# Fourteen weight low parts moved to GpSimd in the conv stage, ten native strips made split strips

## What is computed

```python
h = layer_norm(x) * (1.0 + sc1[:, None]) + sh1[:, None]
proj = h @ w_in[l]
a_val, a_gate, u_pool, gate_a, gate_b = jnp.split(proj, ...)
ya = a_val * jax.nn.sigmoid(a_gate)
ya = causal_dwconv(ya, w_dw_a[l], b_dw_a[l])            # 31 taps, 512 channels
ya = jax.nn.silu(layer_norm(ya, ln_a_g[l], ln_a_b[l]))
ya = ya @ w_pw_a[l]
pooled = causal_multiscale_pool(u_pool)                 # window means over 2, 4, 8, 16 tokens, minus u_pool
yb = jnp.einsum("bsgc,gcd->bsgd", pooled, w_pool[l]).reshape(bsz, s, D_MODEL) * pool_scale[l]
merged = jax.nn.sigmoid(gate_a) * ya + jax.nn.sigmoid(gate_b) * yb
mix = merged @ w_out[l]
```

## Time and profile before

| what | value |
|---|---|
| time, median of three runs | 828.81 us (828.03 to 829.47) |
| time of the profiled execution | 828.66 us |
| its span, first to last instruction | 826.9 us |
| TensorE busy | 811.2 us, 98% of the span |
| VectorE busy | 661.9 us, 80% |
| ScalarE busy | 456.8 us, 55% |
| GpSimd busy | 43.4 us, 5% |
| mean granted TensorE clock | 0.997 |

### The profile page before, as it was taken

One profiled execution on the slowest core, in us unless ns is written; L12 is line 12 of the kernel. 1 busy time (PEld: TensorE's weight loads), 2 busy tenths in 40 slices (PEclk: granted clock), 3 DMA queues, 4 the chain that ended last, 5 costly groups with the idle time before them and its releaser, 6 DMA issues.

```text
span 826.9 us, 14985 instructions
## 1 busy us (share of the span) xinstructions
PE 811.2 (98%) x5394; PEld 738.3 (89%) x5394; DVE 661.9 (80%) x1043; ACT 456.8 (55%) x682; POOL 43.4 (5%) x58
## 2 busy tenths in 40 slices
PE   9999999999999999999999999999999999999995
PEld 9898999988778999999988789988988999999884
DVE  5979887786966887787868778999898888888566
ACT  6464545565646665657565636115744777776440
POOL 0009000000011000000000000060000000000000
PEclk9999999999999999999999999999999999999998
DMA  6957675679735747383749572446571665565641
GB/s 223 363 201 265 209 260 190 238 253 361 256 139 166 261 147 268 119 285 111 271 170 335 183 254 106 136 150 212 187 248 58 229 202 182 192 209 207 201 154 51
DMA packets 49002, 170.57 MB, mean 206 GB/s; under 512 B 6080, under 2 KB 6720, under 8 KB 48960
## 3 DMA queue, kind: packets, MB, share of 16 engines
q1 hardware_dynamic: 40896, 143.23, 50.5%
q10 hardware_dynamic: 8064, 26.78, 9.3%
HBM read 168.93 MB, written 1.06 MB: 206 GB/s over the span
## 4 chain that ended last, share of the span: by engine, by line
PE 77%; DVE 13%; ACT 4%; issue 4%; DMA 1%; DVEq 1%; ACTq 0%
PE bank L498 12%; PE bank L500 12%; PE bank L499 12%; PE bank L566 8%; PE bank L568 8%; PE bank L567 8%; DVE bank L2011 4%; DVE wlo L1521 3%; PE bank L512 2%; PE bank L703 2%; PE bank L704 2%; PE bank L705 2%; DVE ada_raw L1533 1%; PE bank L609 1%; PE bank L852 1%
## 5 line engine op out<-in xcount | busy, mean ns | idle before, releaser
L990 ACT ACTIVATE whi<-raw 128x1024 fp32r<-128x1024 f32 (+1 forms) x236 | 244.2, 1041 | 198.3 <-PE bank L500 85.3
L1521 DVE TENSOR_TENSOR wlo<-raw,whi 128x1024 fp32r<-128x1024 f32 (+1 forms) x236 | 282.9, 1211 | 66.3 <-ACT whi L990 64.2
L498 PE MATMUL bank<-H,whi 128*128 128x256 f32 x816 | 230.8, 283 | 0.6 <-DVE wlo L1521 0.4
L499 PE MATMUL bank<-H,whi 128*128 128x256 f32 x816 | 227.7, 279 | 0.0
L500 PE MATMUL bank<-H,wlo 128*128 128x256 f32 x816 | 227.7, 279 | 0.0
L498 PEld LDWEIGHTS bank<-H,whi 128*128 128x128 f32 x816 | 153.8, 189 | 2.1 <-issue 1.2
L499 PEld LDWEIGHTS bank<-H,whi 128*128 128x128 f32 x816 | 154.7, 190 | 0.1
L500 PEld LDWEIGHTS bank<-H,wlo 128*128 128x128 f32 x816 | 153.2, 188 | 0.0
L566 PE MATMUL bank<-whi,Y 128*128 128x512 f32 x216 | 84.9, 393 | 0.3 <-DVE wlo L1521 0.3
L568 PE MATMUL bank<-whi,Y 128*128 128x512 f32 x216 | 84.3, 390 | 0.0
L567 PE MATMUL bank<-wlo,Y 128*128 128x512 f32 x216 | 84.2, 390 | 0.0
(11 more groups left out here) (265 smaller groups left out, 1315.2 us busy)
## 6 DMA issues: line engine op xcount, KB each, us to landing
ada_raw<-ada_in ACTq DMA_DIRECT2D x48, 512.0 KB, 5.2
raw<-w_head SPq DMA_DIRECT2D x47, 512.0 KB, 4.5
raw<-w_up SPq DMA_DIRECT2D x42, 512.0 KB, 3.5
raw<-w_down SPq DMA_DIRECT2D x22, 512.0 KB, 3.4
raw<-w_uq SPq DMA_DIRECT2D x24, 384.0 KB, 3.1
raw<-w_ret_out SPq DMA_DIRECT2D x16, 512.0 KB, 5.1
raw<-w_mla_gate SPq DMA_DIRECT2D x16, 512.0 KB, 4.6
raw<-w_mla_out SPq DMA_DIRECT2D x16, 512.0 KB, 5.3
```

What stands on the lines that cost most here:

```text
L498: mm(o, whi[:, s, c], a[:, 0, :], start=start, stop=False)
L499: mm(o, whi[:, s, c], a[:, 1, :], start=False, stop=False)
L990: activation(parts_of(b + (per * i if isinstance(i, int) else 0), n)[0], block_in(b, n), ACT.Copy).then_inc(hi_done, 1)
L1521: tt(lo, block_in(b, n), f32(hi), ALU.subtract).then_inc(lo_done, 1)
```

## The change

- WP2, WP3 and WG0 to WG7 become split strips, so that all 20 strips of `B_WP` and `B_WG` are. SyncE loads them without waiting for TensorE.
- Their high parts go to ScalarE, two ahead of each evacuation.
- The low parts of 14 blocks (`GIVEN`: WP2, WP3, WG0 to WG11) go to GpSimd. It makes five, then the window mean over 2, four, the mean over 4, five, and then the means over 8 and 16.
- VectorE loses the low parts of WG8 to WG11 (three between the last taps, one behind `conv_sum`) and the `skip_split`. Behind `conv_sum` it waits until GpSimd has made all of its parts and makes that of WG12; that of WG13 comes behind the centring, and `Sl` moves behind the scaling by `rstd`.
- TensorE does `conv_mean` after WG12 (before: after WG10) and `conv_squares` after WG14 (before: after WG12).
- ScalarE makes `Sh` between the root and the SiLU table (before: between two evacuations).
- The squares lie in `SGT` instead of in `WK`.

```diff
+GIVEN = [B_WP + 2 + j for j in range(14)]
...
             load_all(B_WP, "pool_in")
-            load_plain_loop(B_WG, "gates", 3, 4)
-            load_some(B_WG, "gates", 12, 16)
+            load_all(B_WG, "gates")
...
-                if j < 2:
-                    strip(B_WP + j, halves(b)[j % 2], H)
-                else:
-                    plain_tokens(B_WP + j, halves(b)[j % 2])
-            with pe.Fori(0, 2) as i:
-                for j in range(4):
-                    if j % 2 == 0:
-                        b = free_a(A_WG + j // 2, 2, i)
-                    plain_tokens(B_WG + j, halves(b)[j % 2], 4, i)
-            for j in range(8, 16):
+                strip(B_WP + j, halves(b)[j % 2], H)
+            for j in range(16):
                 if j % 2 == 0:
                     b = free_a(A_WG + j // 2)
                 strip(B_WG + j, halves(b)[j % 2], H)
-                if j == 10:
+                if j == 12:
                     conv_mean()
-                if j == 12:
+                if j == 14:
                     conv_squares()
...
             split(B_WA + 6)
-            skip_split(10)
+            split(B_WA + 7)
             value_gate(3)
             act.wait_ge(pads, 1)
-
+            split(B_WP)
+            split(B_WP + 1)
             evac(B_WP + 1, 0, U[:, 0:2, 16:16 + T], ACT.Copy)
+            split(B_WP + 2)
+            split(B_WP + 3)
             evac(B_WP + 3, 1, U[:, 2:4, 16:16 + T], ACT.Copy)
-            for n in range(3):
+            for n in range(6):
+                split(B_WG + 2 * n)
+                split(B_WG + 2 * n + 1)
                 evac(B_WG + 2 * n + 1, n, pair(G, n), ACT.Sigmoid)
-            act.wait_ge(pooled, 4)
-            activation(Sh, PO, ACT.Copy).then_inc(pooled_hi, 1)
...
             activation(root[:], M3[:, 0:T], ACT.Sqrt, bias=col("ln_eps"), scale=1.0 / (4 * P)).then_inc(root_done, 1)
+            act.wait_ge(pooled, 4)
+            activation(Sh, PO, ACT.Copy).then_inc(pooled_hi, 1)
             table(ACT.Silu)
...
             for k in range(4):
                 if k < 3:
-                    split(B_WG + 5 + k)
-                if k < 3:
                     taps(0, (28 + k,))
...
             tt(CS[:, 0, :], CS[:, 0, :], CS[:, 1, :], ALU.add).then_inc(conv_sum, 1)
-            split(B_WG + 8)
+            dve.wait_ge(lo_done, RING + GIVEN[-1] + 1)
             split(B_WG + 9)
-            split(B_WG + 10)
...
                 stt(pair(Z, p), over(M2[:, 0:T], 2), -1.0 / (4 * P), pair(CO, p), ALU.mult, ALU.add).then_inc(centred, 1)
+            split(B_WG + 10)
...
+            def low_part(b):
+
+                hi, lo = parts_of(b)
+                pool.wait_ge(hi_done, b + 1)
+                gtt(lo, block_in(b, 1024), f32(hi), ALU.subtract).then_inc(lo_done, 1)
...
+            pool.wait_ge(lo_done, RING + GIVEN[0])
+            for n, b in enumerate(GIVEN):
+                low_part(b)
+                if n == 4:
+                    pool.wait_ge(act_free, A_WP + 2 + 2)
+                    window_mean(0)
+                if n == 8:
+                    window_mean(1)
+            window_mean(2)
+            window_mean(3)
```

More of the change, by code:

```diff
@@ L198, in program @@
         SQ = WK[:, 8:16, :]
+        SQC = flat(SGT[:]).rearrange("p (a t) -> p a t", a=4)
         Q, K = WK[:, 0:2, :], WK[:, 2:4, :]
@@ L625, in conv_squares @@
                 for k in range(2):
-                    last = mm(M3[:, 0:T], ones[:], SQ[:, k, :], start=(k == 0), stop=(k == 1))
+                    last = mm(M3[:, 0:T], ones[:], SQC[:, k, :], start=(k == 0), stop=(k == 1))
                 last.then_inc(stat_ready, 1)
@@ L1384, in _ @@
             split(B_WA + 6)
-            skip_split(10)
+            split(B_WA + 7)
             value_gate(3)
             act.wait_ge(pads, 1)
+            split(B_WP)
+            split(B_WP + 1)
             evac(B_WP + 1, 0, U[:, 0:2, 16:16 + T], ACT.Copy)
+            split(B_WP + 2)
+            split(B_WP + 3)
             evac(B_WP + 3, 1, U[:, 2:4, 16:16 + T], ACT.Copy)
-            for n in range(3):
+            for n in range(6):
+                split(B_WG + 2 * n)
+                split(B_WG + 2 * n + 1)
                 evac(B_WG + 2 * n + 1, n, pair(G, n), ACT.Sigmoid)
-            act.wait_ge(pooled, 4)
-            activation(Sh, PO, ACT.Copy).then_inc(pooled_hi, 1)
[L1395 to L1398, removed]
-            split(B_WG + 8)
[L1400 to L1403, removed]
             for p in range(2):
                 act.wait_ge(centred, p + 1)
-                activation(pair(SQ, p), pair(Z, p), ACT.Square).then_inc(sq_ready, 1)
+                activation(pair(SQC, p), pair(Z, p), ACT.Square).then_inc(sq_ready, 1)
             table(ACT.Sqrt)
@@ L2076, in _ @@
                 stt(pair(Z, p), over(M2[:, 0:T], 2), -1.0 / (4 * P), pair(CO, p), ALU.mult, ALU.add).then_inc(centred, 1)
+            split(B_WG + 10)
+            dve.wait_ge(sq_ready, 2)
+            tt(pair(SQC, 0), pair(SQC, 0), pair(SQC, 1), ALU.add).then_inc(conv_sum, 1)
             split(B_WG + 11)
-            dve.wait_ge(sq_ready, 2)
-            tt(pair(SQ, 0), pair(SQ, 0), pair(SQ, 1), ALU.add).then_inc(conv_sum, 1)
-            dve.wait_ge(pooled_hi, 1)
-            tt(Sl, PO, f32(Sh), ALU.subtract).then_inc(pooled_ready, 1)
             split(B_WG + 12)
-            split(B_WG + 13)
             dve.wait_ge(centred, 2)
@@ L2089, in _ @@
                 tt(pair(Z, p), pair(Z, p), over(rstd[:], 2), ALU.mult).then_inc(t_ready, 1)
+            dve.wait_ge(pooled_hi, 1)
+            tt(Sl, PO, f32(Sh), ALU.subtract).then_inc(pooled_ready, 1)
+            split(B_WG + 13)
             split(B_WG + 14)
@@ L2328, in _, with window_mean @@
             pool.wait_ge(pads, 1)
-            pool.wait_ge(act_free, A_WP + 2 + 2)
-            for g, window in enumerate(WINDOWS):
+            def low_part(b):
+                hi, lo = parts_of(b)
+                pool.wait_ge(hi_done, b + 1)
+                gtt(lo, block_in(b, 1024), f32(hi), ALU.subtract).then_inc(lo_done, 1)
+            def window_mean(g):
                 src, shift, n = U[:, g, :], 1, 0
-                while shift < window:
+                while shift < WINDOWS[g]:
                     lo = 2 * shift - 1
@@ L2338, in _ @@
                 chained(gtt(src[:, 16:32], src[:, 16:32], cnt[:, g, :], ALU.mult))
-                chained(gts(src[:, 16:16 + T], src[:, 16:16 + T], 1.0 / window, None, ALU.mult))
+                chained(gts(src[:, 16:16 + T], src[:, 16:16 + T], 1.0 / WINDOWS[g], None, ALU.mult))
                 gtt(PO[:, g, :], src[:, 16:16 + T], U[:, g, 16:16 + T], ALU.subtract).then_inc(pooled, 1)
                 pool.wait_ge(pooled, g + 1)
+            pool.wait_ge(lo_done, RING + GIVEN[0])
[8 more added lines that the diff above has]
+            window_mean(3)
 def _features(a):
```

## The result

| | before | after |
|---|---|---|
| median of 14 runs each, us | 828.57 (824.41 to 829.47) | 832.21 (828.0 to 834.77) |
| ratio, 95% interval | | 1.0045 [1.0032, 1.0059] |
| profiled execution, us | 828.66, span 826.9, clock 0.997 | 829.87, span 828.1, clock 0.995 |
| first strip of the stage to PW0, us | 509.20 to 591.20: 82.00 | 508.18 to 592.46: 84.28 |
| PW0 to the end of the span, us | 235.7 | 235.6 |

The change makes the kernel slower, by 3.6 us between the medians, where 2.3 was forecast. The comparison of the two profiled executions does not show the whole of it. The profiled execution of after is one of the quickest of its 14, and its conv stage began 1.02 us earlier than in the profile of before, in code that the change doesn't touch. So I measure every profile from the stage's first strip to PW0.

A forecast was written before the change was run, and what follows sets the result against it. It took the conv stage as balanced between TensorE and VectorE, with the chain behind the sum of taps deciding. 828.66 + 1.0 (chain) - 0.1 (root to evacuation) + 1.4 (collisions) = 830.96, stated as 831.1 us, range 828.5 to 836.0.

The forecast's parts named there:

- the signs that were named: Conv stage: low parts 2.3 to 2.5 us, second sum ending 569 to 569.5, waits over 2 us, root near 583.
- a sign of being wrong: End of conv stage: root before 580, mean without wait, low parts over 2.6 us, or clock under 1 behind WG12.
- TensorE's 7.2 us come back as waits: Ten exchanged strips' saving returns as waits: 1.5 us WG7, 2 to 4 WG12, 2.5 WG13, about 2 `B_POOL`, 1 PW0.
- GpSimd's pace: GpSimd's low parts: 2.40 us each plus 0.09 between, done with WG11 at 564.5, WG7 1 to 2 us late.
- VectorE 3.4 us earlier: Last conv taps: three low parts leave VectorE, so the second sum ends at 568.3 instead of 571.72.
- The chain +1.0: Behind the sum of taps: two strips now stand in the chain, root at 581.9 instead of 580.90, 1.0 us later.
- the collisions +1.4: SBUF ports: GpSimd's last two means delay VectorE's two sums and WG12's low part, 0.9 to 1.9 us, taken as 1.4.
- From the root to the evacuation: ScalarE, root to WG13's evacuation: `Sh` fills the 1.05 us wait for VectorE's scaling; net about -0.1 us.
- Covers at nothing: ScalarE's ten added high parts and the blocks' loads were costed at nothing, as hidden in existing waits and slack.
- the clock: Rival: TensorE's clock falls at WG12, doubling one strip of the chain, +2.7 us, 833.7 us; chance 0.08.
- The rival "faster": Tail behind the sum of taps keeps its old length, so 3.4 us stay saved, 825.3 us; chance 0.12.

The follow-up runs named there:

- e1_hold: The change plus unread matmuls on TensorE, 9 behind the mean and 13 ahead of the wait for the pooled sums; 830.42 us, ratio 1.0032 to before.
- e3_quiet: The change with GpSimd waiting for the centring before its last two window means; 833.62 us, ratio 1.007 to before.
- e6_hold_all: The change plus unread matmuls in all three TensorE waits: 8 behind WG11's strip, 9 behind the mean, 13 before the pooled matmuls; 826.87 us, ratio 1.0009 to before.
- e11_hold_again: The change with unread matmuls at all three waits again, timed beside the unedited change on one chip; 826.51 us, ratio 1.0015 to before.
- e9_after: The change once more, nothing edited, timed on one chip beside its version with unread matmuls; 831.4 us, ratio 1.0043 to before.
- e2_mean11: The change with TensorE's mean after WG11 instead of after WG12; 828.06 us, ratio 0.9999 to before.
- e12_tail_again: Second run of the change with all sixteen low parts on GpSimd, mean after WG11, squares after WG12, ScalarE's end reordered; 820.92 us, ratio 0.9934 to before.
- e4_given16: The change with GpSimd also making the low parts of WG12 and WG13, mean after WG11, squares after WG13; 828.72 us, ratio 1.0003 to before.
- e7_relief_native: Before with its native strips kept, GpSimd making WG8 to WG11's low parts, mean and squares one strip earlier; 830.41 us, ratio 1.0037 to before.
- e8_mean11_hold: The change with the mean after WG11 and unread matmuls in the three waits (5, 3 and 13); 826.58 us, ratio 0.9992 to before.

## Why the prediction was right, and where it was off

The direction, the place and the mechanism held; the time, 832.2 against 831.1, is 1.1 us above. Of the signs that were named, the low parts (2.37 us), the root (582.98 on before's time scale) and longer sums came; the second sum ended a little early (568.71), the wait before WG12 was under 2 us in this profile, and in e1_hold and e3_quiet the clock fell behind WG12, which the forecast had as a sign of being wrong.

- **TensorE's 7.2 us come back as waits**: 7.5 us in three waits of the profile. Their places: WG12 1.62 (forecast 2 to 4), WG13 2.51 (2.5), `B_POOL` 3.38 (about 2). The wait at WG12 depends on how fast TensorE arrives. The forecast's strip of 2.73 us is that of before's profile, and the profile of after has the slower strips of 2.8 us (last section); with the faster ones the wait was 2.27 us (e3_quiet) and 3.36 us (e1_hold). `B_POOL` did not wait for `Sl`, as the forecast says, but for its own low part, which VectorE makes behind `Sl`. The wait forecast at WG7 (1.5) did not come, and that at PW0 (1) came only with the clock held: 1.05, 1.06 and 0.95 us in e1_hold, e6_hold_all and e11_hold_again.
- **GpSimd's pace**: 2.37 us a part against 2.40 + 0.09. The two instructions follow each other without the 0.09 that I allowed, so the last part was done 54.1 us behind the first strip, not 55.3, and WG7 was not late.
- **VectorE 3.4 us earlier**: 3.3. Taps beside GpSimd cost nothing, as said.
- **The chain +1.0 and the collisions +1.4**: the root comes 73.78 us behind the first strip instead of 71.70, +2.1 against 2.4. The collision term was too large: 0.31 on the second sum and 0.43 on WG12's low part, about 0.75 in all, while the first sum met nothing (e3_quiet shows the same three without GpSimd). In other profiles with the same code it did meet a piece: 0.78 us in e9_after, 0.98 in e11_hold_again, 1.05 in e1_hold, and the whole comes to 0.75 to 1.1 us, against 1.4. The rest of the chain was a little longer than the parts that I added up: 2.81 us from WG12's strip to the mean against 2.73, and 5.57 us for the two strips to the squares against 5.46, for this execution has the slower matmuls of the last section, and before's has the faster.
- **From the root to the evacuation**: 9.43 us against 9.65 before, -0.2 where -0.1 was forecast. That alone puts PW0 at +1.9, and with the clock held at all three waits the stage is 83.87 and 84.22 us, +1.9 and +2.2. The forecast said that `B_POOL`'s strip does not decide; in this profile it did, by 0.4 us, because it ran at half clock. So +2.28 against 2.3 is partly luck: 0.4 too much chain, 0.4 of clock that was not in the sum.
- **Covers at nothing**: ScalarE's high parts and the loads stopped nobody; the tail behind PW0 moved as a whole (235.6 against 235.7 us).
- **The step that was mis-sized is the clock.** I had it as a rival at 0.08 with its place at WG12, not as a term of the sum. It is in nearly every run of the change: clocks of 0.988 to 0.996 in its 26 runs, against 0.996 to 0.998 for before. With the clock held the kernel lies, group against group, 1.7 to 2.6 us above before, around the forecast's 2.3; the fall adds 0.9 to 1.95 us. The prediction had the row that gives it (a fall some 4 us behind TensorE's last matmul), and should have put a part of it into the sum, at all three waits. The Trainium skill ("TensorE: Matmul & The Clock Gate", The HAM clock gate) says that idle gaps bring the lower clock; the traces agree: it fell behind the wait of 3.38 us in after and of 3.36 us in e1_hold. In e9_after it fell behind one of 2.51 us, with 1.62 us idle one strip earlier; in after the same two waits passed at full clock. So it differs from execution to execution, and what decides was not found.
- **The rival "faster"** failed for the reason given, that the order puts a low part and a strip ahead of the mean. One number (e2_mean11) takes this away, and the time is before's again.

## What to carry to other kernels

Work taken off a balanced pair of engines is worth what the chain at the end of the stage lets through: follow the last instructions one by one in the new order and count each strip that has slipped in ahead of a reduction or an activation. After such an exchange look at every engine's order again, and take off the chain what its next reader does not need (`Sh` ahead of the SiLU, a strip ahead of the mean); here this turned 3.6 us above before into 6 to 8 below it. Where an exchange turns TensorE's work into waits, price the clock with it. Cheap unread matmuls in the wait show whether it is the clock, before anything is redesigned.

## What the runs showed of the hardware

**Two speeds of matmuls at one granted clock.** The code of this stretch is the same in both kernels, and the granted clock is 1.00 in both (before, then e1_hold):

```profile
660.00:680.00 20.00, 20.00 (x172) 20.00 (x171) 17.47 (x28) 14.14 (x21) 0.00 (x0) 1.00 0.62 210
```

```profile
660.00:680.00 20.00, 20.00 (x179) 20.00 (x178) 18.69 (x31) 16.48 (x25) 0.00 (x0) 1.00 0.70 234
```

172 or 179 matmuls in 20 us, 4% apart, and from 680 us on every profile has the one or the other. From PW0 to the end of the span it makes 235.7 us against 231.4; e12_tail_again has 179 as well and 231.3 us. This fits the gap between the two groups of times: before's 29 runs beside e9_after are 7 from 823.7 to 825.1 and 22 from 827.2 to 829.7. No profile of before from the lower group was taken.

In the conv stage the same two speeds appear, independently of the later stretch. The profile of before has the faster one there, that of after the slower (before, then after):

```profile
505.00:520.00 15.00, 15.00 (x135) 15.00 (x135) 14.12 (x23) 7.82 (x11) 0.15 (x1) 1.00 0.58 207
505.00:520.00 15.00, 15.00 (x131) 15.00 (x130) 14.09 (x25) 7.35 (x10) 0.15 (x1) 1.00 0.63 217
```

Of the other profiles, e4_given16, e6_hold_all, e7_relief_native and e9_after have the slower one in the stage, the rest the faster. The code of e7_relief_native is that of before up to the mean, and its first strip behind the native ones came 54.21 us behind the stage's first, against 53.62 in before. So a stage of before with the slower matmuls would be some tenths of a us longer than 82.00, by my estimate, and the differences of stages here are no finer than that. What decides the speed was not tried. The faster one seemed more frequent with unread matmuls: lower groups hold 15 of 24 runs of e6_hold_all and e11_hold_again, 5 of 12 of e8_mean11_hold and 2 of 12 of e1_hold, and 28 of 91 of before beside them.

**A subtraction into fp32r on GpSimd.** 128x1024 took 2.37 us, where 2.2 ns an element from the rows of smaller ones into fp32 gave 2.40. So nothing here shows fp32r to be slower.

**The collisions go both ways.** GpSimd's instruction that multiplies 128x16 took 0.22 us alone and 1.09 us beside VectorE's low parts (e3_quiet), as VectorE's low part grew from 1.22 to 1.65 us beside GpSimd.
